# Mixture-of-experts output kept as a running sum in the output rows, one VectorE operation per expert

## The reference, cut to what matters

```python
h2  = rms_norm(x, norm2_g)
gl  = h2 @ w_gr + b_gr                       # 4 groups: the best one, with its softmax share p_g
el  = (h2 @ w_er + b_er)[best group]         # 8 experts in it: the best two
w   = softmax(top two of el) * p_g           # weight of each choice
out = zeros(1024, 1024)
for each expert e, for the tokens that chose it (2048 choices over 32 experts, 64 each on average):
    out[token] += w * ((silu(h2[token] @ w_gate[e]) * (h2[token] @ w_up[e])) @ w_down[e])
return x + out
```

## Time and profile before

| | |
|---|---|
| median of 3 runs | 1523.95 us (1521.49 to 1524.41) |
| profiled execution | 1522.0 us, span 1520.2 us, mean granted clock 0.976 |
| PE / DVE / ACT / POOL busy over the span | 94% / 65% / 52% / 23% |
| DMA in the expert stage, in 40ths of the span | 375 to 392 GB/s |
| chain that ended last, by engine | PE 88%, DVE 3%, DMA 2%, POOL 2% |

### The profile page before, as it was taken

One profiled execution on the slowest core, in us unless ns is written; L12 is line 12 of the kernel. 1 busy time (PEld: TensorE's weight loads), 2 busy tenths in 40 slices (PEclk: granted clock), 3 DMA queues, 4 the chain that ended last, 5 costly groups with the idle time before them and its releaser, 6 DMA issues.

```text
span 1520.2 us, 19135 instructions
## 1 busy us (share of the span) xinstructions
PE 1421.9 (94%) x7264; PEld 1198.1 (79%) x7265; DVE 990.1 (65%) x1409; ACT 789.6 (52%) x1123; POOL 349.3 (23%) x459
## 2 busy tenths in 40 slices
PE   3899999999999999999999969999999999999980
PEld 3888888888888788888888857888888888888860
DVE  4664664674674533434332868888888888888855
ACT  5553353353354322323232437777777777777740
POOL 6334424424433400000001421111211121121110
PEclk9899999999999999999999979999999999999995
DMA  5210210210210233463341259999999999999938
GB/s 164 60 42 1 59 42 1 60 42 1 60 43 1 70 97 84 109 159 84 83 187 56 98 191 375 376 378 388 381 391 378 390 392 383 383 384 381 386 152 331
DMA packets 133196, 290.54 MB, mean 191 GB/s; under 512 B 17008, under 2 KB 95984, under 8 KB 108528
## 3 DMA queue, kind: packets, MB, share of 16 engines
q1 hardware_dynamic: 122736, 268.31, 49.2%
q0 software_dynamic: 9216, 16.80, 2.9%
q10 hardware_dynamic: 1152, 4.19, 0.7%
HBM read 280.87 MB, written 25.17 MB: 201 GB/s over the span
## 4 chain that ended last, share of the span: by engine, by line
PE 88%; DVE 3%; DMA 2%; POOL 2%; issue 1%; ACT 1%; SPq 0%; POOLq 0%; DVEq 0%; ACTq 0%
PE proj L99 17%; PE proj L101 17%; PE proj L100 17%; PE scores L99 7%; PE scores L101 7%; PE scores L100 7%; PE scores L666 2%; PE outs L730 2%; PE scores L547 2%; DMA comb<-y_rows 2%; PE turned L99 1%; PE turned L101 1%; PE turned L100 1%; PE turned L547 1%; PE turned L703 1%
## 5 line engine op out<-in xcount | busy, mean ns | idle before, releaser
L1640 DVE TENSOR_TENSOR w_low<-w_slot,w_high 128x2048 fp32r<-128x2048 f32 x192 | 428.5, 2285 | 20.1 <-ACT w_high L1111 20.0
L1111 ACT ACTIVATE w_high<-w_slot 128x2048 fp32r<-128x2048 f32 x190 | 349.5, 1910 | 2.6 <-DMA w_slot<-in_w_gate 2.6
L99 PE MATMUL proj<-w_high,xeH 128*128 128x512 f32 x512 | 203.5, 397 | 1.8 <-DVE xeL L1708 1.2
L101 PE MATMUL proj<-w_high,xeL 128*128 128x512 f32 x512 | 200.7, 392 | 0.0
L100 PE MATMUL proj<-w_low,xeH 128*128 128x512 f32 x512 | 200.0, 391 | 0.0
L936 ACT ACTIVATE wCH<-wC_in 128x1024 fp32r<-128x1024 f32 x48 | 47.6, 1052 | 154.7 <-DMA wC_in<-in_w_branch_b 154.7
L1324 POOL DMA_INDIRECT y_rows<-y,ids_scatter x32 | 71.6, 2237 | 220.6 <-ACT y L1139 213.9
L1364 DVE TENSOR_TENSOR wCL<-wC_in,wCH 128x1024 fp32r<-128x1024 f32 x48 | 56.9, 1237 | 93.0 <-ACT wCH L936 93.0
L99 PEld LDWEIGHTS proj<-w_high,xeH 128*128 128x128 f32 x512 | 97.0, 189 | 21.7 <-issue 2.4
L101 PEld LDWEIGHTS proj<-w_high,xeL 128*128 128x128 f32 x512 | 96.5, 188 | 20.9
L100 PEld LDWEIGHTS proj<-w_low,xeH 128*128 128x128 f32 x512 | 96.8, 189 | 19.4
(11 more groups left out here) (273 smaller groups left out, 3129.9 us busy)
## 6 DMA issues: line engine op xcount, KB each, us to landing
w_slot<-in_w_gate SPq DMA_DIRECT2D x64, 1024.0 KB, 7.8
w_slot<-in_w_up SPq DMA_DIRECT2D x64, 1024.0 KB, 7.7
w_slot<-in_w_down SPq DMA_DIRECT2D x64, 1024.0 KB, 7.9
wC_in<-in_w_in SPq DMA_DIRECT2D x32, 512.0 KB, 4.9
wB_in<-in_w_in SPq DMA_DIRECT2D x16, 512.0 KB, 5.9
comb<-y_rows SPq DMA_DIRECT2D x16, 512.0 KB, 10.3
wA_in<-in_w_in SPq DMA_DIRECT2D x12, 512.0 KB, 6.3
x_all<-in_x SPq DMA_DIRECT2D x4, 1024.0 KB, 8.2
```

The costliest lines, as they stand in the source:

```text
L99: pe.matmul(out, lh, rh, start=start, stop=False)
L101: return pe.matmul(out, ll, rh, start=False, stop=stop)
L1111: act.activation(w_high[slot][:], w_in6[slot][:], ACT.Copy).then_inc(S["w_split"], 1)
L1640: dve.tensor_tensor(w_low[slot][:], w_in6[slot][:], w_high[slot][:].bitcast(F32), ALU.subtract).then_inc(S["w_lows"], 1)
```

## The change

`x2` is stored to the rows of the output in DRAM as soon as it is known. Each expert then adds its rows there. POOL gathers the rows of its tokens from the output (`cur`, two buffers), DVE forms `SC * weight + cur` in one operation, and POOL scatters the result to the same rows. The slots' weights come from a second table, `w_rows`, made by 16 more small products on PE. As a later expert may hold the same token, the gather for expert e+1 waits until the scatter of e has landed. `y_dram`, the copy on ACT and the whole closing stage go. `x2` needs no place after its store, so there are 10 weight slots.

```diff
-N_SLOTS = 8
+N_SLOTS = 10
 # SP
+            def store_x2(i):
+                sp.dma_start(out_v[:, i, :], x2[:, i, :]).then_inc(S["x2_stored"], DMA)
             for i in range(4):
                 store_h2(i)
+                store_x2(i)
...
             for q in range(4, 6 * N_EXP):
+                if q == 8:
+                    sp.wait_ge(S["x2_stored"], N_TILES * DMA)
                 load_piece(q)
...
-            for i in range(N_TILES):
-                if i >= 4:
-                    sp.wait_ge(S["res_done"], 2 * i - 6)
-                for c in range(2):
-                    sp.dma_start(comb[:, i % 4, c, :], y_v[:, c, i, :]).then_inc(S[f"comb_in{i % 4}"], DMA)
 # PE, after the routing and before the turn of the first expert's rows
+            pe.wait_ge(S["tables_done"], 1)
+            pe.wait_ge(S["route_step"], R_WEIGHTS)
+            for t in range(N_TILES):
+                for c in range(2):
+                    last = pe.matmul(bank(3)[:, 0:32], pick(t, c).bitcast(F32), oh[:, t, c, :],
+                                     start=(t == 0 and c == 0), stop=(t == 7 and c == 1))
+            last.then_inc(S["rows_mm"], 1)
 # ACT
-            def rows_out(e):
-                act.wait_ge(S["w_used"], use_of(e, 5) + 1)
-                if e:
-                    act.wait_ge(S["scattered"], DMA * e)
-                act.activation(y[:], SC[:, 1, :], ACT.Copy).then_inc(S["y_out"], 1)
...
-                if e:
-                    rows_out(e - 1)
                 hid_high(e + 1)
...
-            for i in range(N_TILES):
-                act.wait_ge(S["res_done"], 2 * i + 2)
-                act.dma_start(out_v[:, i, :], res[:, i % 4, :]).then_inc(S[f"out_stored{i % 4}"], DMA)
 # POOL
+            def gather_cur(e):
+                pool.indirect_dma_start(out=cur[:, e % 2, :], out_offset=None, in_=out_rows,
+                                        in_offset=bass.IndirectOffsetOnAxis(ap=ids_rows[:, e:e + 1], axis=0),
+                                        bounds_check=1023, oob_is_err=False).then_inc(S["cur_landed"], DMA)
...
             gather_rows(0)
-            for e in (1, 2):
-                pool.wait_ge(S["xeT_done"], e)
-                gather_rows(e)
+            pool.wait_ge(S["xeT_done"], 1)
+            gather_rows(1)
+            pool.wait_ge(S["x2_stored"], N_TILES * DMA)
+            pool.wait_ge(S["rows_weighed"], 1)
+            gather_cur(0)
+            pool.wait_ge(S["xeT_done"], 2)
+            gather_rows(2)
             for e in range(N_EXP):
                 if e + 3 < N_EXP:
                     pool.wait_ge(S["xeT_done"], e + 3)
                     gather_rows(e + 3)
-                pool.wait_ge(S["y_out"], e + 1 + FREE)
                 scatter_rows(e)              # waits for y_out of e itself
-            pool.wait_ge(S["scattered"], DMA * N_EXP)
+                pool.wait_ge(S["scattered"], DMA * (e + 1))
+                if e + 1 < N_EXP:
+                    gather_cur(e + 1)
 # DVE, routing
+            route(dve.tensor_tensor(oh[:]..., oh[:]..., wsel[:]..., ALU.mult))      # 128 x 512
+            dve.wait_ge(S["rows_mm"], 10)
+            dve.tensor_copy(w_rows[:, 0:32], bank(3)[:, 0:32]).then_inc(S["rows_weighed"], 1)
 # DVE, expert stage
+            def rows_out(e):
+                dve.wait_ge(S["w_used"], use_of(e, 5) + 1)
+                dve.wait_ge(S["cur_landed"], DMA * (e + 1))
+                if e:
+                    dve.wait_ge(S["scattered"], DMA * e)
+                dve.scalar_tensor_tensor(y[:], SC[:, 1, :], w_rows[:, e:e + 1], cur[:, e % 2, :], ALU.mult, ALU.add
+                                         ).then_inc(S["y_out"], 1)
...
+                if e:
+                    rows_out(e - 1)
                 hid_low(e + 1)
+            rows_out(N_EXP - 1)
...
-            for i in range(N_TILES):
-                ...
-                dve.scalar_tensor_tensor(res[:, b, :], comb[:, b, 0, :], wsel[:, 0, i:i + 1], x2[:, i, :], ALU.mult, ALU.add
-                                         ).then_inc(S["res_done"], 1)
```

More of the change, by code:

```diff
@@ L32 @@
 DMA = 16
-R_DIFFS = 91
-NO_ROW = 2048
-N_SLOTS = 8
+R_DIFFS, R_WEIGHTS = 90, 99
+NO_ROW = 1024
+N_SLOTS = 10
 def use_of(e, c):
@@ L58 @@
     ("freq", 72), ("ret_q", 4), ("ret_k", 4), ("ret_g", 4), ("ret_ginv", 4), ("minus_half", 16), ("half_pi", 1),
-    ("strict", 128), ("ones", 128), ("iota", 256), ("token_m", 16), ("rev_grp", 4),
+    ("strict", 128), ("ones", 128), ("iota", 256), ("token_m", 8), ("rev_grp", 4),
 ]
@@ L269, in decoder_layer, with pick @@
         eidx = rt("eidx", [P, 8, 2])
[L270 to L273, removed]
         posm = rt("posm", [P, 2, 32])
         pos = rt("pos", [P, 8, 2])
[L276 to L279, removed]
+        wsel = rt("wsel", [P, 8, 2])
+        cur_ids = rt("cur_ids", [P, 1], I32)
+        cur_w = rt("cur_w", [P, 1])
+        rdead = region(cur_at, oTH_end)
+        logits = rdead("logits", [P, N_TILES, 36])
+        count_masks = rdead("count_masks", [P, 256], F32R)
+        oh = rdead("oh", [P, 8, 2, 32])
+        mask = rdead("mask", [P, 8, 32], F32R)
+        before = rdead("before", [P, 9, 32], F32R)
+        pick_lo = rt("pick_lo", [P, 2, 2, 128], F32R)
+        keyid1 = rt("keyid1", [P, 8, 2, 32], F32R)
+        pick_hi = sb("pick_hi", [P, 6, 2, 128], F32R, at=R_A + 18 * KIB)
+        cur = sb("cur", [P, 2, 1024], F32, at=cur_at)
+        def pick(t, c):
+            return pick_lo[:, t, c, :] if t < 2 else pick_hi[:, t - 2, c, :]
         rs = region(R_WORK + 16 * KIB, R_WORK + 20 * KIB)
-        ids_scatter = rs("ids_scatter", [P, 256], I32)
-        ids_gather = rs("ids_gather", [P, 256], I32)
+        ids_rows = rs("ids_rows", [P, 256], I32)
+        w_rows = rs("w_rows", [P, 256])
         counts_f = rs("counts_f", [P, 33])
@@ L302, in decoder_layer @@
         keyid = [ro(f"keyid{i}", [P, 256], F32R) for i in range(2)]
-        slot_at = [R_HT, R_HT + 16 * KIB, R_WORK, R_B, R_B + 16 * KIB, R_OT, R_OT + 16 * KIB, merged_at[1]]
+        key_w = [ro(f"key_w{i}", [P, 256]) for i in range(2)]
+        slot_at = [R_HT, R_HT + 16 * KIB, R_WORK, R_B, R_B + 16 * KIB, R_OT, R_OT + 16 * KIB, merged_at[1],
+                   R_HT + 32 * KIB, R_HT + 48 * KIB]
         w_in6 = [sb(f"w_slot{i}", [P, 2048], F32, at=slot_at[i]) for i in range(N_SLOTS)]
@@ L325, in decoder_layer @@
         h2_dram = nc.dram_tensor("h2_rows", (1024, 1024), F32, kind="Internal").ap()
-        y_dram = nc.dram_tensor("y_rows", (2048, 1024), F32, kind="Internal").ap()
+        out_rows = T["out"][0]
         w_in_v = T["w_in"][0].rearrange("(k p) c -> p k c", p=P)
@@ L531, in _ @@
             overflow(sp, loads_again)
-            sp.wait_ge(S["rows_stored"], 1)
-            for i in range(N_TILES):
-                if i >= 4:
-                    sp.wait_ge(S["res_done"], 2 * i - 6)
-                for c in range(2):
-                    sp.dma_start(comb[:, i % 4, c, :], y_v[:, c, i, :]).then_inc(S[f"comb_in{i % 4}"], DMA)
-            for b in range(4):
-                sp.wait_ge(S[f"out_stored{b}"], DMA * N_TILES // 4)
+            sp.wait_ge(S["x2_stored"], N_TILES * DMA)
         def turn_rows(pe, src_rows, dst, step, n):
@@ L838, in rows_of @@
                 for c in range(2):
-                    last = pe.matmul(bank(3)[:, 0:32], pick[:, t % 2, c, :], keyid1[:, t, c, :],
+                    last = pe.matmul(bank(3)[:, 0:32], pick(t, c), keyid1[:, t, c, :],
                                      start=(t == 0 and c == 0), stop=(t == 7 and c == 1))
@@ L1169, in block_steps @@
                 act.wait_ge(S["w_used"], n * 6 + (6 * N_EXP + 6))
-                act.activation(y[:], SC[:, 1, :], ACT.Copy).then_inc(S["y_out"], 1)
+                act.activation(y[:], SC[:, 1, :], ACT.Copy, scale=cur_w[:, 0:1]).then_inc(S["y_out"], 1)
             act.wait_ge(S["scattered"], DMA * N_EXP)
             overflow(act, block_steps)
-            for i in range(N_TILES):
-                act.wait_ge(S["res_done"], 2 * i + 2)
-                act.dma_start(out_v[:, i, :], res[:, i % 4, :]).then_inc(S[f"out_stored{i % 4}"], DMA)
         @block.gpsimd
@@ L1294, in _ @@
                 pool.tensor_tensor(rstd2[:, i:i + 1], ms2[:, 1, i:i + 1], mhalf[:, 0:1], ALU.pow).then_inc(S["n2_rstd"], 1)
[L1297 to L1309, removed]
             pool.wait_ge(S["lg_done"], 16)
@@ L1342, in block_moves @@
                 col = pool.snap(b * N_EXP + e)
[L1343 to L1346, removed]
+                results, rows, back = pool.snap(n + (N_EXP + 1) + FREE), pool.snap(n * DMA + DMA * (N_EXP + 1)), pool.snap(n * DMA + DMA * (N_EXP + 1))
+                pool.tensor_copy(cur_ids[:], ids_rows[:, DS(col, 1)]).then_inc(S["idx_copied"], 1)
+                pool.tensor_copy(cur_w[:], w_rows[:, DS(col, 1)]).then_inc(S["idx_copied"], 1)
+                pool.wait_ge(S["idx_copied"], 2)
+                pool.indirect_dma_start(out=xe[:], out_offset=None, in_=h2_dram,
```

(33 more changed lines are left out.)

49 lines of the change are left out of this document (24 added, 25 removed).

## The result

| | before | changed |
|---|---|---|
| median | 1522.87 us (4 runs) | 1578.36 us (1570.53 to 1581.9, 4 runs) |
| ratio | | 1.0357, 95% interval 1.0316 to 1.0399 |
| profiled execution, its span | 1522.0, 1520.2 | 1581.9, 1579.8 |

The direction and the mechanism came out as forecast, at twice the size (+55 us against +28); the time lies inside the stated range. The profiled execution is the slowest of the four, so the figures that follow from its trace lean to the slow side by 3.5 us in all.

A forecast was written before the change was run, and what follows sets the result against it. PE bounds the kernel at 17.78 us per expert; the new ring would replace it. 944.0, 29 turns of 19.7, two last turns and the end give span 1547.8, +27.6; median 1551.5 us, range 1511 to 1596.

The forecast's parts named there:

- end of the first operation: First DVE add of the expert stage: 941.74 plus 1.3 for the operation and 1.0 for PE's later start, 944.0.
- 29 turns: Expert stage: 29 turns of 19.7 us bring y_out of expert 29 to 1515.3; each us of a turn is worth 29.
- the last two turns: End of the expert stage, few or no weight loads beside them: 15.5 and 11.2 us.
- from the last operation to the end: After the last DVE add: handover 0.8, scatter 4.0 and 1.0 for POOL's last steps, 5.8 us.
- The ring: Per expert: DVE operation, scatter, its landing, next gather, its landing; 21.4 us under load against a 17.78 us period.
- I take 19.7: The turn chosen between the linear rule's 20.2 and the 16.1 from the stage's start, nearer the former.
- The linear rule: Expert stage: turn interpolated between 11.2 us without weight loads and 21.4 under them, by load share; gives 20.2.
- the two early landings of the earlier trace: At the expert stage's start, with fewer loads queued: 7.6 and 5.5 us, a turn of 16.1.
- The rival with nothing shrunk: Expert stage: landings don't shorten as the period grows, 21.4 us per turn, span 1597, median 1601; chance 0.18.
- 8 like them took 1.08: Routing's end on PE: basis for pricing 16 new products at 2.2 us, 4.3 at half clock; 1.0 of delay taken.
- Traffic and slots: Expert stage: cur gathers cost 0 to 0.6 us per period, counted only through landings; 10 slots gain 0.
- the 19.0 that the prediction gave for rows on half of the engines: Expert stage: period if 64 rows load half the DMA engines and those are full; top of the DMA rival, chance 0.18.

The follow-up runs named there:

- e1: Changed kernel with experts taken from each routing group in turn and the gather of cur waiting one scatter further back: 1516.65 us, 0.9962 of before.
- e2: Changed kernel with the gather of xe issued earlier, ahead of the wait for the scatter's landing, which is kept: 1583.74 us, 1.0422 of before.
- e5: Changed kernel with only the order of experts of e1, the gather still waiting for the scatter just before it: 1582.17 us, 1.0368 of before.
- e8: e4 with PE's products for the slots' weights, the w_rows copy and the first cur gather moved later: 1497.31 us, 0.983 of before.
- e3: e1 with cur gathered for the first two positions alone, so the sum over experts is left out: 1496.6 us, 0.9828 of before.
- e4: e1 with each expert's 64 rows spread over all 128 partitions, not the first 64: 1500.31 us, 0.9858 of before.
- e7: The kernel before, with the rows spread over all 128 partitions: 1520.5 us, 0.9981 of before.
- e6: Changed kernel with the rows spread over all 128 partitions, the wait and natural order kept: 1557.0 us, 1.0216 of before.

## Why the prediction was right, and where it was short

The profiled span was forecast as 1547.8 and is 1579.8. The sum's terms:

| term | forecast | measured | difference |
|---|---|---|---|
| end of the first operation | 944.0 | 947.2 | +3.2 |
| 29 turns | 571.3 (19.7 each) | 594.7 (20.51) | +23.4 |
| the last two turns | 26.7 | 24.8 | -1.9 |
| from the last operation to the end | 5.8 | 13.2 | +7.4 |

- **The ring** is the cause, and e1, e2 and e5 show it: the time falls by 62 us with the wait moved, and doesn't without. The operation and all handovers were within 0.2 us of the forecast. The mis-sized step is "I take 19.7": how far landings shrink as the period grows. The gather did not shrink at all (8.32 against the 8.3 of `xe` in the kernel before; `xe` itself, now right behind it, went to 10.3), the scatter by a tenth. The linear rule gave 20.2, 0.3 too low; leaning to the two early landings of the earlier trace rows made it 0.8 too low, and 29 turns multiply that. The first turn alone took 25.05 us, since its scatter's issue on POOL took 7.2 us. The rival with nothing shrunk (21.4) was as near by the turn, 0.9 too high, and nearer by the time: 1597 of span and 1601 us by the median, as against the forecast's 1547.8 and 1551.5, for 1579.8 and 1578.36. Its reason, that a landing depends little on how long the queue of loads is, is what e1's landings bear out (10.3 us for the scatter, with loads that take 21.9).
- **The start.** 16 products were priced from "8 like them took 1.08". The row's x8 counts instructions, and each fp32 product has two, as the changed kernel's row shows:

```profile
897.62 1.89 PE L875 MATMUL scores<-oh,pick_lo 128*128 128x32 f32 x8 [3.09 <-DVE oh L1694]
899.32 5.31 PE L875 MATMUL scores<-oh,pick_hi 128*128 128x32 f32 x24
904.44 1.95 PE L912 MATMUL scores<-consts,xe 128*128 128x128 f32 x8
```

  32 instructions at the lower clock (0.50 granted) take 7.0 us, and the first turn of rows starts at 904.44, where it was 900.10; 1.0 was forecast. e8, where they run later, at a granted clock of 1.00, in 3.7 us, gets 3 us of it back.
- **The end.** The "about 1 us" for POOL's last steps missed its drain, the last row of POOL's program:

```profile
L105 POOLq DRAIN  x1: 7915/7915/7915, 1571.7 to 1571.7; - x1
```

  The kernel before has one of 5.4 us too, but from 1484 on, beside the closing stage, which hid it. That cover went with the stage.
- **DVE's operation**: 1.3 forecast, 1.28 measured, and free of cost by itself (e3 at PE's pace).
- **Traffic and slots.** Beside the ring the traffic seems to have hidden, as summed (DMA was at a share of 0.92 and 347 GB/s); no run takes it away with the ring kept. Without the ring the period is 18.8 us (e1), near the 19.0 that the prediction gave for rows on half of the engines, and e4 takes the difference away by spreading the rows. That the figure is so near has some luck in it. The sum asked for engines that are full in the kernel before, and they weren't: its loads landed in 7.8 us, not 21.9, and spreading its rows left its period as it was (e7). By the same prices that kernel would need 0.917 x 17.78 + 2 x 1.24 = 18.8 us and runs at 17.77. 385 GB/s was the wrong floor for DMA as a whole: e4 moves 404.
- **The stores of x2** cost nothing that the window of 850 to 880 shows.

## What to carry to other kernels

Where a step turns a batch of independent scatters into read, add and write back, sum the round trip of one item (issue, landing, handover, landing, operation) and hold it against the period; if it doesn't fit, the saved stage can be more than paid back: here a closing stage of 37.3 us went, and 29 turns of 20.51 us in place of 17.77 cost 79. Look then for an order in which neighbours don't depend on each other: here, one expert of each routing group in turn was enough. A share of 1.0 on the DMA engines says that they are occupied, not that they are evenly loaded, and a stage that is removed may have hidden something that starts before it ends.

## What was not expected of the hardware

- POOL's drain at the end grows with the indirect DMAs that it issued: 5.43 us after 64 (before), 5.54 after 66 (e3), 7.92 after 96 (changed, e1, e2, e4), about 0.08 us for each.
- A scatter's issue occupies POOL for 2.86 us in the changed kernel, where the same rows took 2.30 in the kernel before, and for 1.0 in the last two experts, where DVE idles. Its end goes with DVE's low parts: it comes 0.9 us after the end of the one in whose midst the issue started. The first scatter's lasts 7.23 us, to 0.9 us after the third of three in a row; in e6 five of the 28 from expert 1 to 28 take 7.27. Why it is one low part in some cases and three in others stays open.

```profile
948.02 7.23 POOL L1320 DMA_INDIRECT out<-y,ids_rows  x1 [9.52 <-DVE y L1750]
```
```profile
947.68 6.68 DVE L1652 TENSOR_TENSOR w_low<-w_slot,w_high 128x2048 fp32r<-128x2048 f32 x3
```

- The granted clock of PE fell to 0.94 to 0.98 in stretches of 100 us of the changed kernel's expert stage, where PE waited several us at a time for rows or low parts; it was 1.00 before and is 1.00 in e1 and e4.
